# One more f tile of an FFN by seven products: two plain tiles in place of three

## The reference, cut to what matters

```python
FFN_HIDDEN = 2816          # 22 tiles of 128
h = rmsnorm(x, g_ffn_pre)
f = (jax.nn.silu(h @ w_ffn_gate) * (h @ w_ffn_up)) @ w_ffn_down
```

## Time and profile before

| what | us |
|---|---|
| median of 3 runs | 992.07 |
| the three runs | 992.04, 992.07, 994.11 |
| time of the profiled execution | 993.12 |
| its span, first to last instruction | 991.5 |
| PE busy in the span | 974.4 (98%) |
| DVE busy | 632.0 (64%) |
| ACT busy | 396.9 (40%) |

### The profile page before, as it was taken

How to read it: one execution, slowest core, us unless ns; L and a number is a source line. 1 busy time by engine, 2 the same in 40 slices (tenths; PEclk the granted TensorE clock), 3 DMA queues, 4 the chain that set the end, 5 groups by cost and what they waited for, 6 DMA issues and landing times.

```text
span 991.5 us, 19157 instructions
## 1 busy us (share of the span) xinstructions
PE 974.4 (98%) x7256; PEld 951.2 (96%) x7256; DVE 632.0 (64%) x1244; ACT 396.9 (40%) x695; POOL 88.3 (9%) x140
## 2 busy tenths in 40 slices
PE   6999999999999999999999999999999999999997
PEld 5999999999999999999999999999999999999997
DVE  5545666757665633435457799625997469965862
ACT  5324434435243522222454555423553234443352
POOL 1032212212110000010002000000000000030100
PEclk9999999999999999999999999999999999999999
DMA  8434221221222232245603523521334213365211
GB/s 213 126 114 130 83 69 54 63 74 54 68 70 64 76 88 81 74 124 172 192 3 112 207 62 110 149 64 44 97 112 118 80 47 110 95 210 179 86 51 47
DMA packets 166198, 98.47 MB, mean 99 GB/s; under 512 B 14656, under 2 KB 162528, under 8 KB 165872
## 3 DMA queue, kind: packets, MB, share of 16 engines
q1 hardware_dynamic: 159904, 79.19, 28.2%
q0 software_dynamic: 4336, 16.67, 4.7%
q10 hardware_dynamic: 1888, 1.64, 0.6%
HBM read 86.79 MB, written 10.75 MB: 98 GB/s over the span
## 4 chain that ended last, share of the span: by engine, by line
PE 92%; DVE 4%; issue 2%; ACT 1%; DMA 0%; POOL 0%; DVEq 0%; ACTq 0%
PE acc L679 35%; PE acc L942 11%; PE acc L943 11%; PE acc L944 11%; PE small L942 6%; PE small L943 6%; PE small L944 6%; PE small L811 1%; PE small L828 1%; PE small L857 1%; PE small L861 1%; PE small L859 1%; PE small L759 1%; ACT prob L1182 1%; PE small L869 1%
## 5 line engine op out<-in xcount | busy, mean ns | idle before, releaser
L679 PE MATMUL acc<-xh,whi 128*128 128x288 f32 x736 | 163.3, 303 | 1.6 <-DVE wlo L1604 1.5
L679 PE MATMUL acc<-xl,whi 128*128 128x288 f32 x736 | 157.0, 294 | 0.0
L679 PE MATMUL acc<-xh,wlo 128*128 128x288 f32 x736 | 156.9, 294 | 0.0
L1122 ACT ACTIVATE whi<-raw 128x1024 fp32r<-128x1024 f32 (+1 forms) x62 | 62.1, 1001 | 198.3 <-PE acc L679 198.3
L1604 DVE TENSOR_TENSOR wlo<-raw,whi 128x1024 fp32r<-128x1024 f32 (+1 forms) x64 | 74.2, 1160 | 81.1 <-ACT whi L1122 77.7
L679 PEld LDWEIGHTS acc<-xh,whi 128*128 128x128 f32 x736 | 116.8, 189 | 6.2 <-issue 5.0
L679 PEld LDWEIGHTS acc<-xl,whi 128*128 128x128 f32 x736 | 118.1, 188 | 0.0
L679 PEld LDWEIGHTS acc<-xh,wlo 128*128 128x128 f32 x736 | 117.7, 188 | 0.0
L1916 DVE TENSOR_TENSOR wlo<-raw,whi 128x512 fp32r<-128x512 f32 (+2 forms) x93 | 81.0, 872 | 48.8 <-ACT whi L1333 33.1
L942 PE MATMUL acc<-yh,whi 128*128 128x288 f32 x360 | 107.3, 298 | 0.3 <-DVE wlo L1897 0.3
L944 PE MATMUL acc<-yh,wlo 128*128 128x288 f32 x360 | 106.1, 295 | 0.0
(11 more groups left out here) (314 smaller groups left out, 2370.5 us busy)
## 6 DMA issues: line engine op xcount, KB each, us to landing
raw<-in_w_in SPq DMA_DIRECT2D x92, 256.0 KB, 3.1
raw<-in_w_ffn_gate SPq DMA_DIRECT2D x44, 256.0 KB, 3.3
raw<-in_w_ffn_up SPq DMA_DIRECT2D x44, 256.0 KB, 4.1
raw<-in_w_ffn_down SPq DMA_DIRECT2D x32, 256.0 KB, 3.5
res<-x_scratch POOLq DMA_DIRECT2D x16, 288.0 KB, 4.1
raw<-in_w_branch_ret SPq DMA_DIRECT2D x16, 256.0 KB, 2.9
raw<-in_w_out SPq DMA_DIRECT2D x16, 256.0 KB, 4.6
raw<-in_w_ffn_down SPq DMA_DIRECT2D x16, 192.0 KB, 3.7
```

Source lines behind the costliest of these rows:

```text
L679: ins = nc.tensor.matmul(acc[:, a, hf, 0:HALF], w[:, s, at:at + P], x(k)[:, hf * HALF:(hf + 1) * HALF], start=first and n == 0 and m == 0, ...
L1122: nc.scalar.activation(whi[:, s, 0:n], raw[:, s, 0:n], ACT.Copy).then_inc(hi_ready, 1)
```

## The change

`PLAIN` goes from 3 to 2. Units `ffn` 4 and 5 (96 matmuls in banks 2 to 5) disappear, and tile 2 goes by seven products (84 matmuls in banks 0 to 6). They stand on PE right behind units 2 and 3 of half 1. The sums of y that they read are made at another place of DVE's and ACT's lists, interleaved with the operands of tile 2's products and with the silus and f tiles of units 0 to 3, half 1.

```diff
-PLAIN = 3
+PLAIN = 2
...
             several("ffn", ((0, 1), (1, 1)), yh, yl, ready=lambda k: pe.wait_ge(y_lo, KD + k + 1))
             several("ffn", ((2, 1), (3, 1)), yh, yl)
-            for n in (4, 5):
-                for h in range(2):
-                    half_unit("ffn", n, h, yh, yl)
...
             gate_silu(1, 0)
             f_half(1, 0)
-            hi(("ffn", 4))
-            hi(("ffn", 5))
...
+            hi(("prod", PLAIN, PA0))
+            hi(("prod", PLAIN, PS1))
+            t_high(0)
+            t_high(1)
             gate_silu(0, 1)
             f_half(0, 1)
-            t_high(0)
-            t_high(1)
+            hi(("prod", PLAIN, PS2))
+            hi(("prod", PLAIN, PA1))
+            hi(("prod", PLAIN, PS4))
             gate_silu(1, 1)
+            t_high(2)
             f_half(1, 1)
-            t_high(2)
+            hi(("prod", PLAIN, PS3))
             t_high(3)
...
+            hi(("prod", PLAIN, PB1))
...
-            first_products(PLAIN, 0)
-            first_products(PLAIN, 1)
-            f_half(2, 0, 4)
-            f_half(2, 1, 5)
+            product_operand(PLAIN, PA0)
+            t_sum(0)
+            t_sum(1)
+            t_sum(2)
+            t_sum(3)
+            product_operand(PLAIN, PS1)
+            t_low(0)
+            f_half(0, 1, 2)
+            f_half_low(0, 1, 2)
+            product_operand(PLAIN, PS2)
+            t_low(1)
+            product_operand(PLAIN, PA1)
+            product_operand(PLAIN, PS4)
+            f_half(1, 1, 3)
+            f_half_low(1, 1, 3)
             t_low(2)
-            first_products(PLAIN, 2)
+            product_operand(PLAIN, PS3)
             t_low(3)
-            first_products(PLAIN, 3)
...
+            product_operand(PLAIN, PB1)
```

More of the change, by code:

```diff
@@ L1070, in f_wait @@
             def f_wait(i):
-                pe.wait_ge(f_lo, (3, 4, 6)[i] if i < PLAIN else PLAIN + i + 1)
+                pe.wait_ge(f_lo, (3, 4)[i] if i < PLAIN else PLAIN + i + 1)
             for g, tiles in enumerate(GROUPS):
@@ L1447, in _ @@
             f_half(1, 0)
-            hi(("ffn", 4))
-            hi(("ffn", 5))
-            gate_silu(0, 1)
-            f_half(0, 1)
-            t_high(0)
-            t_high(1)
-            gate_silu(1, 1)
-            f_half(1, 1)
-            t_high(2)
-            t_high(3)
             def first_products(i, n):
@@ L1463, in first_products @@
                     hi(("prod", i, t))
[L1465 to L1468, removed]
-            first_products(PLAIN, 3)
-            f_half(2, 0)
-            f_half(2, 1)
+            hi(("prod", PLAIN, PA0))
+            hi(("prod", PLAIN, PS1))
+            t_high(0)
+            t_high(1)
+            gate_silu(0, 1)
+            f_half(0, 1)
+            hi(("prod", PLAIN, PS2))
+            hi(("prod", PLAIN, PA1))
+            hi(("prod", PLAIN, PS4))
+            gate_silu(1, 1)
+            t_high(2)
+            f_half(1, 1)
+            hi(("prod", PLAIN, PS3))
+            t_high(3)
+            hi(("prod", PLAIN, PB1))
             def copy_out(e, dst):
@@ L2071, in _ @@
             f_half_low(1, 0, 1)
[L2072 to L2083, removed]
             def sum_of(i, t):
@@ L2114, in first_products @@
                     product_operand(i, t)
-            first_products(PLAIN, 0)
-            first_products(PLAIN, 1)
-            f_half(2, 0, 4)
-            f_half(2, 1, 5)
+            product_operand(PLAIN, PA0)
[13 more added lines that the diff above has]
+            f_half_low(1, 1, 3)
             t_low(2)
-            first_products(PLAIN, 2)
+            product_operand(PLAIN, PS3)
             t_low(3)
-            first_products(PLAIN, 3)
-            f_half_low(2, 0, 4)
-            f_half_low(2, 1, 5)
+            product_operand(PLAIN, PB1)
             def f_low(i):
```

## The result

| | kernel before | changed kernel |
|---|---|---|
| median us (four runs each) | 992.06 | 1000.15 |
| lowest and highest | 992.00 to 994.11 | 999.83 to 1002.18 |
| profiled execution, its span | 993.12, 991.5 | 999.95, 998.3 |
| ratio, 95% interval | | 1.0081, 1.0062 to 1.0099 |

A forecast was written before the change was run, and what follows sets the result against it. PE, busy 98% of the span, was taken as the bound. Waits of 6.5 and 1.4 plus 0.2 for restarts, less 1.6 of matmuls, plus 0.8 for the clock made +7.3 on 992.07: 999.4 us, range 998.0 to 1001.6.

The forecast's parts named there:

- The cover: Tile 2's plain units gave 12.75 us between PE's last use of banks 0 and 1 and their next use.
- The first wait: At tile 2's first product PA0, PE waits 6.5 us for ACT's silu to read bank 0, until 567.8.
- The second wait: At product PS1, PE waits 1.4 us for DVE's f half to read bank 1, until 570.9.
- the second queue: DVE's list up to its read of bank 1, said to hold PE until about 570 even with ACT free.
- The clock: PE's clock falls in the first wait, slowing matmuls behind it: 0.8 us taken, between 0 and 2.3.
- the restart: PE's first matmul behind each of two waits takes 0.1 us longer, 0.2 in the sum.
- the bounds of 0 and 2.3: Low clock's cost: 0 if back by 570.9, 2.3 us if low for twice the start's 3.9 us.
- Rival 1: Banks 0 and 1 read as soon as full, waits short: 992.4 us (0.05) or a gain (0.03); chance 0.08.
- only the sums: With both banks read early, DVE's sums alone hold PE at PS1: 1.9 us plus 0.1, against 1.6 gained.
- If the sums were 2 us earlier: With banks read early and sums 2 us earlier as well, nothing at tile 2 would wait: 990.5 us.
- Rival 2: Clock stays at 1.2 GHz through the rest of tile 2: +8 in place of +0.8, 1006.6 us; chance 0.05.
- Rival 3: DVE falls behind in the product stage, PE waits 1 to 3 us at tile 3: 1000.4 to 1002.4; chance 0.05.

The follow-up runs named there:

- experiment 2: Changed kernel with the silus and f halves that read the banks put first on ACT's and DVE's lists; median 996.15 us, ratio 1.0030 to the kernel before.
- experiment 4: Changed kernel without the sums of y, products reading quarters of y itself (another output); median 991.88 us, ratio 0.9987 to the kernel before.
- experiment 3: Changed kernel with 46 additional unread matmuls on PE in the place of the wait; median 998.86 us, ratio 1.0063 to the kernel before.
- Experiment 1: Changed kernel with the silu that frees bank 0 moved ahead of three weight operands on ACT; median 1001.45 us, ratio 1.0085 to the kernel before.
- experiment 6: Experiment 5 with one sum of y and one weight sum made by GpSimd, lists reordered; median 998.56 us, ratio 1.0061 to the kernel before.
- experiment 8: Experiment 7 with three high parts of y put between ACT's ple copies, lists reordered; median 990.80 us, ratio 0.9978 to the kernel before.
- Experiment 5: Changed kernel with both lists in order of need and high parts released earlier, same work per engine; median 995.49 us, ratio 1.0028 to the kernel before.
- experiment 7: Changed kernel with tile 2's four weight sums made in DVE's earlier idle time, lists following experiment 5; median 992.93 us, ratio 0.9999 to the kernel before.

## Why the prediction was right, and where it was off

**The cover (right).** The 12.75 us of two plain units were also the time in which banks 0 and 1 were read and the sums of y were made. That step made the sign. Experiments 2 and 4 confirm both halves of it: with the readers ahead 4.6 us come back (1.35 of them the clock's, by experiment 3), without the sums all of it. Tile 3 then comes 0.66 sooner than before.

**The first wait (right, 6.5).** The profile says 6.53. Laid out from durations of the trace before, the steps gave 566.85 for `hi` PS4, 567.37 for the silu and 567.8 for PA0. They came at 566.62, 567.16 and 567.70, and with the 0.28 by which the changed profile is early at the common matmul each is within 0.2 us.

**The second wait (right as a mechanism, unseen in the trace).** `f_half(1, 1)` was put at 570.40 and came at 570.12. The changed kernel shows no idle time at PS1, since PA0 took 3.02 us at the low clock; the clock paragraph said so. Experiment 1 shows the wait (1.62) and the claim that the second queue holds PE until about 570 in any case; experiment 3 shows it at full clock (1.19).

**The clock (right in kind, too small in size).** This is the term that was mis-sized: 0.8 forecast, 1.35 by experiment 3. On PS1 and PS2 it is 1.43 (4.62 less 3.19), of which 0.1 is the restart that the sum has as a term of its own. The median of 1000.15 lies 0.75 above 999.4, and most of that is this term.

I took the kernel's start as the nearer measure, 3 to 4 us of matmuls at the low level. Here it was 6.0 us behind the wait, and 9.1 in experiment 1. And the start was read too short. I counted from its first matmuls of 128x288, but PE's transposes ahead of them have the slow pace too (PE's timeline in the kernel before):

```profile
6.22 5.43 PE L759 MATMUL small<-tab,x_row 128*128 128x128 f32 x20 [0.26 <-DVE gains L1617]
...
14.74 1.35 PE L759 MATMUL small<-tab,x_row 128*128 128x128 f32 x5
...
17.31 0.80 PE L759 MATMUL small<-tab,x_row 128*128 128x128 f32 x5
```

One takes 0.27 us in the first row and 0.26 in the second (the next row starts at 16.02), but 0.15 in the third (the next starts at 18.04). So the slow pace lasted from 6.2 to about 16.9, over 10 us. (PEclk is shown as 1.00 in this stretch, so it is the pace that tells.) In the other profiled executions it ended between 16.6 (experiment 6) and 22.4 (experiment 8), so the start could not size this term to half a us. That the bounds of 0 and 2.3 held it is partly luck, since 2.3 was twice a length that had been read too short.

The low clock in the wait also agrees with the rule of the Trainium skill that the prediction cited ("TensorE: Matmul & The Clock Gate", "HAM oscillation — how this bites in real kernels"): PEclk was 0.50 when PA0 began, and without that rule's mechanism the sum would have been 6.5, where experiment 3, which takes it away, has 6.6.

**Rival 1 (rightly unlikely, but its price was wrong).** It said that with both readers in time only the sums would hold PE, for 2.0 us against 1.6 of gain, 992.4 in all. Experiment 2 put the readers in time and stood at +3.35, not at +0.4. The step that failed is "only the sums": it took DVE's sums as the whole queue, and left out that the bank reads and the weight operands are on the same engine and only change places with them. Experiment 5 gives the floor of that load, +1.24 at tile 3 with DVE busy for every microsecond. "If the sums were 2 us earlier" is near experiment 7, which moved 2.4 us of DVE up, for -0.96 in place of -1.6.

**Rival 2 and rival 3.** The clock came back as PS1 ended, within tile 2. Rival 3, the product stage that pays later, did not happen in the changed kernel: DVE's lead at tile 3 was 5.2 us, where the prediction had 3.8. DVE was there as laid out (576.48, and with the 0.28 that is 576.76 against 576.8), and PE came 1.4 us later than 580.6, with the clock's term among it. But its mechanism is real, and PE's long wait had hidden it. As soon as PE loses little at tile 2 (experiments 5 and 7), DVE is late by 0.3 at tile 3 and by 0.4 to 0.6 at the last f tile.

## What to carry to other kernels

Before work is taken off the busiest engine, ask what ran under it: here 1.6 us of matmuls saved uncovered 12.75 us in which two other engines read banks and made operands. Write down each queue up to the instruction that frees the next bank; an in-order engine lets nothing past, and moving one reader ahead is worth nothing if a second queue holds the same engine (experiment 1). When the order is right, the load of the next engine is the floor, and what helps is work moved up into its idle stretches (experiment 7), not a better order and not a helper that the busy engine has to wait for (experiment 6).

## What the runs showed of the hardware

- PE's clock stood at 1.2 GHz for 10.2 us both times that it fell in the middle of the kernel, in the changed kernel (563.5 to 573.7) and in experiment 1 (565.9 to 576.1). The wait ended 4.2 us after the fall in the one and 1.1 us after it in the other, so the earlier restart bought no earlier full clock. The fall itself came 2.3 us after PE's last matmul in the one and 3.6 us after it in the other, and in experiment 2 PE idled for 3.00 us with PEclk at 1.00.
- At the kernel's start PE's slow pace (0.24 us for a matmul of 128x288) ended at 16.6 to 22.4 us in the eleven profiled executions, with PE at work since about 6.1. The common matmul lies at 540.79 where the slow pace ended first and at 542.86 where it ended last. No run tells whether the one makes the other, but 2 us are more than most of what is compared here, which is why all is counted from that matmul.
- DVE and GpSimd kept each other out on element-wise instructions with two SBUF inputs: 3.26 us in place of 1.05 for two DVE instructions, 3.44 us for a GpSimd sum of 512 elements where one of 1152 took 2.72. In both cases GpSimd got through where DVE had a gap.
- A single wait of PE costs about 0.1 us beyond its length: the first matmul behind it is shown 0.37 to 0.40 long in place of 0.29.
